# Dense products of a two-layer hybrid trunk: 520 tokens in parts of 240 and 280 instead of 260 and 260, five matmuls instead of six for each 128 by 128 weight block

## The chip, the cores and the metric

The kernel runs on one core of a Trainium2 chip. The metric is the device time of one execution in microseconds (us). The engines are named as in the profile: PE (TensorE; PEld is its loading of weights), DVE (VectorE), ACT (ScalarE), POOL (GpSimd), SP (SyncE). SBUF is the on-chip memory with 128 partitions, PSUM the memory that PE writes, here 8 banks of 512 float32 in each partition.

## The reference

Two decoder layers over 512 prompt tokens and 8 sample tokens, together 520 columns, all in float32. Cut to the dense products, which are what the change touches:

```python
def decoder_layer(x, ple, w, ...):
    h = rmsnorm(x, w['norm_ffn1'])
    x = x + 0.5 * swiglu(h, w['ffn1_w1'], w['ffn1_w3'], w['ffn1_w2'])   # 1024 -> 2816 (twice) -> 1024
    h = rmsnorm(x, w['norm_mix'])
    u = h @ w['w_in']                                                   # 1024 -> 5640
    dn_qkv, dn_z, dn_b, dn_a, da_q, da_k, da_v, gate_a, gate_b = split_in(u)
    ya = gated_delta_branch(...)                                        # convolution, L2 norms, scan
    yb = differential_attention(...)
    m = sigmoid(gate_a) * (ya @ w['w_a']) + sigmoid(gate_b) * (yb @ w['w_b'])
    x = x + m @ w['w_o']
    h = rmsnorm(x, w['norm_ffn2'])
    x = x + 0.5 * swiglu(h, w['ffn2_w1'], w['ffn2_w3'], w['ffn2_w2'])
    gate = sigmoid(rmsnorm(x, w['norm_ple']) @ w['w_ple_gate'])
    return x + gate * (ple @ w['w_ple'])
```

## The kernel before, in words

Activations stand transposed in SBUF, features on the partitions and the 520 tokens along the row: `X` is [128, 8, 520]. Every dense product is made of three products in the format fp32r: a float32 number is split into a high part (the same number written as fp32r) and a low part (what is left), for the activations (`Hh`, `Hl`; `Gh`, `Gl` of the FFN's hidden values; `Yh`, `Yl`; `Mh`, `Ml`; `PTh`, `PTl`) and for the weights (`whi`, `wlo`). The result is high weight by high activation, plus high weight by low activation, plus low weight by high activation, summed in PSUM. The 520 tokens do not fit one bank, so they are cut into two halves of `HT = 260`, each in a bank of its own. One weight block of 128 by 128 thus takes a set of six matmuls of 260 columns (`product`, L603 to L618; `block_low`, L643 to L667). `pair(b)` is the view of the two halves in banks b and b + 1, and `halves` cuts an SBUF row in the same way.

A weight block of the program is 128 x 2048 (8 chunks k by 256 columns): 16 sets, 96 matmuls, four banks. Two such blocks alternate between banks 0 to 3 and banks 4 to 7 (`block8`). In `block_low`, where other work needs banks 4 to 7, the two halves of a block use banks 0, 1 and banks 2, 3 and are released one by one (`half_done`, `half_evac`). The FFN's down products have 11 chunks by 128 columns, two of them to an output.

The order on each engine is written out by hand and every dependency is a semaphore. For each weight block SP loads `raw`, ACT writes `whi` (`hi`), DVE or POOL writes `wlo` (`lo`, L1665 on DVE) and PE waits for `split_done` (`split_ready`). PE also waits for `evac` (`banks_ready`) before it reuses banks. DVE empties the banks, in nearly all places by one instruction per output chunk: PSUM times `R`, the reciprocal root of the norm, into SBUF. Layer by layer the stages are: FFN 1 up (22 blocks, `ffn`), FFN 1 down (16 blocks of 66 matmuls), the convolution's six blocks of w_in (`to_u`, then nine DVE instructions per block, L1750 on), eight blocks by `block_low` with the L2 norms between them (`low_u`, L1780; `l2_norms`, L1795), the scan and the attention, eight gate blocks by `block_low` (`gate_half`, `head_norm`), w_a and w_b (`AB`, eight products of 48 matmuls), w_o (4 blocks), FFN 2, and the per-layer embedding (four products of 24 matmuls with `PTh`, then four blocks with the gate). DVE's `acc` holds the running sum of squares for the norms; `norm_rec` clears it after each use. The last chunk of layer 1 has its own loop (L1180 to L1187), by halves of 260.

Of the kernel before, what the change touches and what calls it, by code (L numbers as in the profile page):

```python
# [2353 lines left out]
```

## Time and profile before

| | |
|---|---|
| median of 3 runs | 2753.1 us (2751.6 to 2753.88) |
| the profiled execution (its span, first to last instruction) | 2749.5 us |
| PE matmuls | 2704.5 us busy, 98%, 23840 instructions |
| PE weight loads | 2566.3 us busy, 93%, 23840 |
| DVE | 1349.4 us, 49%, 1662 |
| ACT | 1021.9 us, 37%, 1168 |
| POOL | 241.2 us, 9%, 150 |
| DMA | 33.2% of 16 engines' span, 303.81 MB |

A matmul's time in the profile is its way from issue to the last result and overlaps the next ones: 282 ns each, although they start some 119 ns apart. So the mean duration is no cost; the distance from start to start is, and that is read from how many matmuls fill a stretch in which PE never idles. The 3.6 us between the profiled span and the median of the runs lie outside the instructions or between executions.

### The profile page before, as it was taken

How to read it: one execution, taken by the hardware profiler on the slowest of the kernel's cores; microseconds unless marked ns; L12 is line 12 of the kernel's file. 1: busy time of each engine (PE TensorE's matmuls, PEld its weight loads, DVE VectorE, ACT ScalarE, POOL GpSimd, SP SyncE). 2: the span in 40 equal slices, each digit the busy share in tenths (PEclk: the TensorE clock that was granted, in tenths of full speed). 3: DMA queues.
4: the chain of work that ended last, by engine and by line, in shares of the span. 5: the costliest groups of instructions: out<-in, count | busy, mean ns of one | idle time of the engine just before them, and what ended most of it. 6: DMA issues, size and time to landing. Idle time of an engine off the chain costs nothing.

```text
span 2749.5 us, 56360 instructions
## 1 busy us (share of the span) xinstructions
PE 2704.5 (98%) x23840; PEld 2566.3 (93%) x23840; DVE 1349.4 (49%) x1662; ACT 1021.9 (37%) x1168; POOL 241.2 (9%) x150
## 2 busy tenths in 40 slices
PE   8999999999999999999999999999999999999997
PEld 8999999976699999999999999999657999999997
DVE  5333347644676533333653333567356665333336
ACT  5333223412563333332343332333135534333223
POOL 0111000421000011100001100013210000111000
PEclk9999999999999999999999999999999999999998
DMA  4222232277422222222322222323873222222221
GB/s 159 93 92 73 94 119 95 94 228 249 151 81 89 93 92 92 87 85 89 108 92 92 92 79 93 124 91 100 269 240 104 93 93 81 93 92 85 87 95 66
DMA packets 119534, 303.81 MB, mean 110 GB/s; under 512 B 14946, under 2 KB 25186, under 8 KB 118882
## 3 DMA queue, kind: packets, MB, share of 16 engines
q1 hardware_dynamic: 119394, 301.79, 33.2%
q8 instruction: 106, 1.74, 0.3%
q14 instruction: 34, 0.28, 0.0%
HBM read 290.30 MB, written 11.44 MB: 110 GB/s over the span
## 4 chain that ended last, share of the span: by engine, by line
PE 93%; DVE 3%; ACT 2%; DVEq 2%; issue 1%; DMA 0%; SPq 0%; POOLq 0%; ACTq 0%
PE ps L614 69%; PE ps L662 13%; PE ps L829 2%; PE ps L916 1%; PE ps L982 1%; ACT sc L1230 1%; PE ps L897 1%; PE ps L883 1%; PE ps L715 1%; PE ps L1128 1%; DVEq L1799 0%; PE ps L964 0%; PE ps L710 0%; PE ps L935 0%; DVEq L1991 0%
## 5 line engine op out<-in xcount | busy, mean ns | idle before, releaser
L614 PE MATMUL ps<-Hh,whi 128*128 128x260 f32 x3440 | 691.9, 283 | 11.7 <-DVE Hl L1725 10.1
L614 PE MATMUL ps<-Hl,whi 128*128 128x260 f32 x3440 | 690.0, 282 | 0.0
L614 PE MATMUL ps<-Hh,wlo 128*128 128x260 f32 x3440 | 689.0, 282 | 0.0
L1230 ACT ACTIVATE whi<-raw 128x2048 fp32r<-128x2048 f32 (+2 forms) x225 | 396.0, 1760 | 780.2 <-PE ps L614 670.6
L1659 DVE TENSOR_TENSOR wlo<-raw,whi 128x2048 fp32r<-128x2048 f32 (+2 forms) x213 | 444.2, 2085 | 292.3 <-ACT whi L1230 292.2
L614 PEld LDWEIGHTS ps<-Hh,whi 128*128 128x128 f32 x3440 | 527.9, 188 | 12.8 <-issue 10.1
L614 PEld LDWEIGHTS ps<-Hl,whi 128*128 128x128 f32 x3440 | 530.2, 189 | 0.0
L614 PEld LDWEIGHTS ps<-Hh,wlo 128*128 128x128 f32 x3440 | 529.2, 188 | 0.0
L1230 ACT ACT_TABLE_LOAD x163 | 209.1, 1283 | 304.0 <-PE ps L614 233.4
L1659 DVE TENSOR_TENSOR ta<-ps,R 128x520 f32<-128x520 f32 x88 | 61.6, 700 | 475.8 <-PE ps L614 474.7
L614 PE MATMUL ps<-Gh,whi 128*128 128x260 f32 x1408 | 283.7, 283 | 0.0
L614 PE MATMUL ps<-Gh,wlo 128*128 128x260 f32 x1408 | 283.4, 282 | 0.0
L614 PE MATMUL ps<-Gl,whi 128*128 128x260 f32 x1408 | 282.7, 282 | 0.0
L1600 POOL TENSOR_TENSOR Gl<-tb,Gh 128x520 f32 x88 | 115.3, 1310 | 1594.1 <-ACT Gh L1230 1594.1
L614 PEld LDWEIGHTS ps<-Gl,whi 128*128 128x128 f32 x1408 | 217.2, 188 | 0.0
L614 PEld LDWEIGHTS ps<-Gh,whi 128*128 128x128 f32 x1408 | 216.8, 188 | 0.0
L614 PEld LDWEIGHTS ps<-Gh,wlo 128*128 128x128 f32 x1408 | 216.7, 188 | 0.0
L662 PE MATMUL ps<-Hh,whi 128*128 128x260 f32 x1024 | 212.8, 289 | 0.3 <-DVE U L1659 0.3
L662 PE MATMUL ps<-Hh,wlo 128*128 128x260 f32 x1024 | 206.1, 283 | 0.0
L662 PE MATMUL ps<-Hl,whi 128*128 128x260 f32 x1024 | 205.8, 283 | 0.0
L662 PEld LDWEIGHTS ps<-Hh,whi 128*128 128x128 f32 x1024 | 159.6, 189 | 4.5 <-issue 2.9
L662 PEld LDWEIGHTS ps<-Hh,wlo 128*128 128x128 f32 x1024 | 157.7, 188 | 0.0
(275 smaller groups left out, 2933.9 us busy)
## 6 DMA issues: line engine op xcount, KB each, us to landing
raw<-in_ffn_up SPq DMA_DIRECT2D x176, 512.0 KB, 4.2
raw<-in_ffn_down SPq DMA_DIRECT2D x128, 352.0 KB, 3.3
kb<-in_cache_k SPq DMA_DIRECT2D x128, 256.0 KB, 3.7
kb<-in_cache_v SPq DMA_DIRECT2D x128, 256.0 KB, 3.8
raw<-in_w_in SPq DMA_DIRECT2D x56, 512.0 KB, 4.4
raw<-in_w_gate SPq DMA_DIRECT2D x32, 512.0 KB, 4.8
raw<-in_w_ab SPq DMA_DIRECT2D x16, 512.0 KB, 4.4
raw<-in_w_o SPq DMA_DIRECT2D x16, 512.0 KB, 4.4
```

Source lines behind the costliest of these rows:

```text
L614: last = nc.tensor.matmul(ps[:, bank + 2 * m + c, 0:HT], w, x[:, k0 + k, c * HT:(c + 1) * HT], start=starts and k == 0 and n == 0, stop=st ...
L662: last = nc.tensor.matmul(ps[:, 2 * m + c, 0:HT], w, x[:, k, c * HT:(c + 1) * HT], start=k == 0 and t == 0, stop=k == KD - 1 and t == 2)
L715: return nc.tensor.matmul(out, in_, CC[0:rows, C_ID:C_ID + rows], start=True, stop=True)
L829: last = nc.tensor.matmul(ps[part(h % 2), bank, cell(x, h)], lhs[part(h % 2), cell(x, h)], rhs(part(h % 2), cell(x, h)), start=x == 0 and ...
L883: last = nc.tensor.matmul(ps[:, 3, o:o + 2], st[b][:, s, h * P:(h + 1) * P], dq[:, 4 * b + s, h, :], start=True, stop=True)
L897: nc.tensor.matmul(ps[:, 3, :], bkm[:, s, :], Uz[:, :, :].rearrange("p h c -> p (h c)"), start=True, stop=True).then_inc(s_pe.on(f"o{b}{s} ...
L916: last = nc.tensor.matmul(ps[32 * h:32 * h + 32, 6, :].rearrange("p (g k) -> p g k", g=4), qz[:, s * P + 32 * h:s * P + 32 * h + 32], kb[t ...
L982: last = nc.tensor.matmul(ps[:, 7, t * P:SEQ], vtok[:, h % 2, t * P:(t + 1) * P], aT[:, t, t * P:SEQ], start=t == 0, stop=t == 3)
L1128: last = nc.tensor.matmul(ps[:, 4 + 2 * (k % 2) + c, 0:HT], ones, tb[:, k % 2, c * HT:(c + 1) * HT], start=True, stop=True)
L1230: return nc.scalar.activation(out, in_, func, **kw)
L1600: nc.gpsimd.tensor_tensor(col(Gl, 2 * i + p), tb[:, p, :], col(Gh, 2 * i + p).bitcast(F32), ALU.subtract).then_inc(gl_done, 1)
L1659: return V.tensor_tensor(out, a_, b_, op)
```

## The change

Tokens are cut into the first `N0 = 240` and the other 280. The high and the low activations of a product now stand in one tensor (`Hs`, `Gs`, `YMs`, `PTs`, at the addresses that they had), so one matmul of 480 columns takes the first 240 tokens of both: the high weight by high and by low activation, to two neighbouring stretches of one bank. Only one of the two stretches is the place where the sum is built; the other is added to it later, by DVE. The set of one 128 by 128 weight block is five matmuls with 480 + 280 + 280 + 240 + 280 = 1560 columns, where it was 6 x 260 = 1560. The 480-column matmul is the first of a set that opens an accumulation and the last of all others. `fold` is the new DVE work: it copies the stretch of 240 columns (for one or two output chunks) from PSUM to SBUF and adds it to the sum in PSUM, with a drain after each. Where the result goes to `X` (down products, w_o) there is no `fold` but one more addition of 240 columns per chunk. `acc` serves as `fold`'s buffer between norms, so its clearing moves from `norm_rec` to the places before the next sum. The main row of 520 tokens is now contiguous over two banks (columns 272 to 511 and 0 to 279). Nothing is changed on SP, POOL or in the number of ACT instructions. The last chunk's own loop (L1180) is left as it was.

```diff
+N0 = 240
+BANK = 512
+AT = BANK - N0
...
         def pair(b):
-            return ps[:, b:b + 2, 0:HT]
...
+            return ps[:, b:b + 2, :].rearrange("p a c -> p (a c)")[:, AT:AT + T]
...
+            def five(h, l, x, bank, start, stop):
+
+                xs, hk, lk = x
+                low, n1 = abs(lk - hk), T - N0
+                first, top_ = min(hk, lk), AT - N0 if hk < lk else AT
+
+                def both():
+                    return nc.tensor.matmul(ps[:, bank, AT - N0:BANK].rearrange("p (a c) -> p a c", a=2), h,
+                                            xs[:, first:first + low + 1:low, 0:N0], start=start, stop=stop)
+
+                if start:
+                    last = both()
+                nc.tensor.matmul(ps[:, bank + 1, 0:n1], h, xs[:, hk, N0:T], start=start, stop=False)
+                nc.tensor.matmul(ps[:, bank + 1, 0:n1], h, xs[:, lk, N0:T], start=False, stop=False)
+                nc.tensor.matmul(ps[:, bank, top_:top_ + N0], l, xs[:, hk, 0:N0], start=False, stop=False)
+                last = nc.tensor.matmul(ps[:, bank + 1, 0:n1], l, xs[:, hk, N0:T], start=False, stop=stop)
+                if not start:
+                    last = both()
+                return last
...
-                        for n, (w, x) in enumerate(((h, rh), (h, rl), (l, rh))):
-                            for c in range(2):
-                                last = nc.tensor.matmul(ps[:, bank + 2 * m + c, 0:HT], w,
-                                                        x[:, k0 + k, c * HT:(c + 1) * HT],
-                                                        start=starts and k == 0 and n == 0,
-                                                        stop=stops and k == ks - 1 and n == 2)
+                        last = five(whi[:, slot, o:o + P], wlo[:, slot, o:o + P], rx(k0 + k), bank + 2 * m,
+                                    starts and k == 0, stops and k == ks - 1)
...
+            low_parts = acc[:, 0:2 * N0].rearrange("p (a c) -> p a c", a=2)
+
+            def fold(b, n=1, by=low_parts):
+
+                x = ps[:, b:b + 2 * n:2, AT:BANK]
+                V.tensor_copy(by[:, 0:n, :], ps[:, b:b + 2 * n:2, AT - N0:AT])
+                dve.drain()
+                TT(x, x, by[:, 0:n, :], ALU.add)
+                dve.drain()
...
                         done(L, nb + m)
 
+                        fold(4 * p, 2)
                         dve.wait_ge(gl_done, L * 2 * KF + m + (hid * KF + 1))
-                        TT(halves(ta[:, p, :]), pair(4 * p), halves(R[:, :]), ALU.mult).then_inc(ta_ready, 1)
-                        TT(halves(tb[:, p, :]), pair(4 * p + 2), halves(R[:, :]), ALU.mult).then_inc(evac, 1)
+                        TT(ta[:, p, :], pair(4 * p), R[:, :], ALU.mult).then_inc(ta_ready, 1)
+                        TT(tb[:, p, :], pair(4 * p + 2), R[:, :], ALU.mult).then_inc(evac, 1)
...
-                        V.scalar_tensor_tensor(out=halves(Xc(m)), in0=pair(4 * p), scalar=0.5, in1=halves(Xc(m)),
+                        x0 = X[:, bass.ds(m, 1), 0:N0].rearrange("p o t -> p (o t)")
+                        V.scalar_tensor_tensor(out=x0, in0=ps[:, 4 * p, AT - N0:AT], scalar=0.5, in1=x0, op0=ALU.mult, op1=ALU.add)
+                        dve.drain()
+                        V.scalar_tensor_tensor(out=Xc(m), in0=pair(4 * p), scalar=0.5, in1=Xc(m),
                                                op0=ALU.mult, op1=ALU.add).then_inc(evac, 1)
...
-                        TT(halves(U[:, u + m, :]), pair(2 * m), halves(R[:, :]), ALU.mult).then_inc(evac if m else half_evac, 1)
+                        fold(2 * m)
+                        TT(U[:, u + m, :], pair(2 * m), R[:, :], ALU.mult).then_inc(evac if m else half_evac, 1)
```

`fold(4 * p, 2)` or `fold(2 * m)` is added in the same way in `to_u`, `gate_half`, the w_a and w_b loop, the embedding's products and its gate.

PE, the first weight block of the program, around the sum of squares (`acc` by the ones in `CC`): before,

```order
L614 MATMUL ps<-Hl,whi 128x260 x2
L614 MATMUL ps<-Hh,wlo 128x260 x2
L674 MATMUL ps<-acc,CC 128x260 x2
L614 MATMUL ps<-Hh,whi 128x260 x2
L614 MATMUL ps<-Hl,whi 128x260 x2
```

and of the change:

```order
L616 MATMUL ps<-Hs,whi 128x480
L708 MATMUL ps<-acc,CC 128x240
L708 MATMUL ps<-acc,CC 128x280
L621 MATMUL ps<-Hs,whi 128x280
L622 MATMUL ps<-Hs,whi 128x280
L623 MATMUL ps<-Hs,wlo 128x240
L624 MATMUL ps<-Hs,wlo 128x280
```

Three pairs of 260 columns became one matmul of 480, three of 280 and one of 240.

DVE, in the stretch of the L2 norms (`ta` holds a root, `U` the projections): before,

```order
L1828 TENSOR_SCALAR gg<-ax 128x20
L1798 RECIPROCAL ta<-ta 128x520
L1800 SCALAR_TENSOR_TENSOR U<-U,ta 128x520
L1798 RECIPROCAL ta<-ta 128x520
L1800 SCALAR_TENSOR_TENSOR U<-U,ta 128x520
L1659 TENSOR_TENSOR U<-ps,R 128x520 x2
L1659 TENSOR_TENSOR gg<-gg,sp 128x20
```

and of the change:

```order
L1850 SCALAR_TENSOR_TENSOR U<-U,ta 128x520
L1706 COPY acc<-ps 128x240
L1691 TENSOR_TENSOR ps<-ps,acc 128x240
L1691 TENSOR_TENSOR U<-ps,R 128x520
L1706 COPY acc<-ps 128x240
L1691 TENSOR_TENSOR ps<-ps,acc 128x240
L1691 TENSOR_TENSOR U<-ps,R 128x520
L1691 TENSOR_TENSOR gg<-gg,sp 128x20
```

Each emptying of a half block is now three instructions, and they still stand behind the same two reciprocals.

## Rows read from the trace of the kernel before

**Rows 1.** The page: busy time of each engine; the chain, by engine

```profile
PE 2704.5 (98%) x23840; PEld 2566.3 (93%) x23840; DVE 1349.4 (49%) x1662; ACT 1021.9 (37%) x1168; POOL 241.2 (9%) x150
PE 93%; DVE 3%; ACT 2%; DVEq 2%; issue 1%; DMA 0%; SPq 0%; POOLq 0%; ACTq 0%
```

**Rows 2.** The page's groups of matmuls (count; busy us, mean ns; idle before)

```profile
L614 PE MATMUL ps<-Hh,wlo 128*128 128x260 f32 x3440 | 689.0, 282 | 0.0
...
L614 PE MATMUL ps<-Gh,wlo 128*128 128x260 f32 x1408 | 283.4, 282 | 0.0
...
L662 PE MATMUL ps<-Hh,wlo 128*128 128x260 f32 x1024 | 206.1, 283 | 0.0
```

**Rows 3.** The chain in order of time: start us, us, what

```profile
1383.40 378.30 PE ps L614 x3168
...
2304.62 387.07 PE ps L614 x3240
```

**Rows 4.** Timeline of PE and PEld, short streams and plain float32: start, length

```profile
588.85 0.97 PEld L883 LDWEIGHTS ps<-dq,st 128*128 128x128 f32 x8 [0.84 <-issue]
...
507.61 1.04 PE L733 MATMUL ps<-tb,CC 128*128 128x260 f32 x4
```

**Rows 5.** Groups of those: duration min/median/max of loads and matmuls

```profile
L883 PEld LDWEIGHTS ps<-dq,st x128: 186/192/192, 584.8 to 1988.9; 128*128 128x128 f32 x128
...
L733 PE MATMUL ps<-tb,CC x64: 381/382/487, 493.0 to 1901.5; 128*128 128x260 f32 x64
```

**Rows 6.** Groups of DVE by form, for the price of `fold`

```profile
L1892 DVE COPY Tm<-ps 128x512 f32<-128x512 f32 x20 | 13.8, 692 | 43.0 <-PE ps L829 42.9
...
L1659 DVE TENSOR_TENSOR st<-st,ps 128x512 f32<-128x512 f32 x16 | 11.0, 687 | 16.4 <-PE ps L897 16.4
...
L1975 DVE COPY Pz<-ps 128x256 f32<-128x256 f32 x2 | 0.8, 424 | 4.6 <-PE ps L926 4.6
```

**Rows 7.** Timeline of DVE, FFN up and its end (start, length, idle before)

```profile
266.07 0.70 DVE L1659 TENSOR_TENSOR ta<-ps,R 128x520 f32<-128x520 f32 x1 [5.11 <-PE ps L614]
...
267.93 2.29 DVE L1659 TENSOR_TENSOR wlo<-raw,whi 128x2048 fp32r<-128x2048 f32 x1 [0.56 <-ACT whi L1230]
```

**Rows 8.** Timeline of POOL, the last low part of the hidden values

```profile
271.96 1.32 POOL L1600 TENSOR_TENSOR Gl<-tb,Gh 128x520 f32 x1 [8.67 <-ACT Gh L1230]
```

**Rows 9.** Timeline of DVE, the convolution's blocks

```profile
428.18 1.31 DVE L1659 TENSOR_TENSOR U<-ps,R 128x520 f32 x2 [0.28 <-PE ps L614]
...
439.58 1.30 DVE L1659 TENSOR_TENSOR U<-ps,R 128x520 f32 x2 [1.79 <-PE ps L614]
```

**Rows 10.** Timeline of DVE and then PE, the L2 norms

```profile
502.33 4.13 DVE L1828 TENSOR_SCALAR gg<-ax 128x20 f32<-128x20 f32 x1 [0.50 <-issue]
...
514.57 1.30 DVE L1659 TENSOR_TENSOR U<-ps,R 128x520 f32<-128x520 f32 x2
...
515.41 0.48 PE L662 MATMUL ps<-Hh,whi 128*128 128x260 f32 x2 [0.16 <-DVE U L1659]
```

**Rows 11.** Busy us by stretch: PE, PEld, DVE, ACT, POOL; clock; DMA

```profile
500.00:556.00 56.00, 55.84 (x456) 53.54 (x452) 48.96 (x50) 25.41 (x32) 18.42 (x4) 1.00 0.21 77
```

**Rows 12.** Timeline of DVE and PE from the last gate to w_a and w_b

```profile
845.56 2.29 DVE L1659 TENSOR_TENSOR wlo<-raw,whi 128x2048 fp32r<-128x2048 f32 x1
...
847.90 0.50 PE L614 MATMUL ps<-Yh,whi 128*128 128x260 f32 x2 [0.33 <-DVE wlo L1659]
```

**Rows 13.** Timeline of DVE, two products of w_b in a row

```profile
859.71 1.31 DVE L1659 TENSOR_TENSOR sg<-ps,sg 128x520 f32<-128x520 f32 x2 [4.46 <-PE ps L614]
...
868.17 2.28 DVE L1659 TENSOR_TENSOR wlo<-raw,whi 128x2048 fp32r<-128x2048 f32 x1
```

**Rows 14.** Timeline of DVE, the embedding's products

```profile
1321.35 2.29 DVE L1659 TENSOR_TENSOR wlo<-raw,whi 128x2048 fp32r<-128x2048 f32 x1 [0.64 <-ACT whi L1230]
```

**Rows 15.** Timeline of PE and DVE, layer 0 to 1, then the end

```profile
1377.95 0.51 PE L614 MATMUL ps<-Hh,whi 128*128 128x260 f32 x2 [0.21 <-DVE Hl L2196]
...
2719.80 1.31 DVE L1659 TENSOR_TENSOR pg<-ps,R 128x520 f32<-128x520 f32 x2 [2.52 <-PE ps L614]
```

More of the change, by code:

```diff
@@ L659, in block_low @@
                             pe.wait_ge(hl_done, L * KD + k + 1)
-                        for t, (w, x) in enumerate(((h, Hh), (h, Hl), (l, Hh))):
-                            for c in range(2):
-                                last = nc.tensor.matmul(ps[:, 2 * m + c, 0:HT], w, x[:, k, c * HT:(c + 1) * HT],
-                                                        start=k == 0 and t == 0, stop=k == KD - 1 and t == 2)
+                        last = five(h, l, Hx(k), 2 * m, k == 0, k == KD - 1)
                     last.then_inc(block_done if m else half_done, 1)
@@ L673, in norm_sum @@
                 for c in range(2):
-                    last = nc.tensor.matmul(ps[:, 6 + c, 0:HT], ones, acc[:, c * HT:(c + 1) * HT], start=True, stop=True)
+                    last = nc.tensor.matmul(cut(6, c), ones, acc[:, tok(c)], start=True, stop=True)
                 last.then_inc(sum_ready, 1)
@@ L1239, in norm_root @@
                 act.wait_ge(sum_ready, L * NORMS + (nj + 1))
-                A_(halves(R[:, :]), pair(6), ACT.Sqrt, scale=1.0 / D, bias=eps).then_inc(rt_ready, 1)
+                A_(R[:, :], pair(6), ACT.Sqrt, scale=1.0 / D, bias=eps).then_inc(rt_ready, 1)
             def x_ready(L, u):
@@ L1323, in l2_root @@
                         act.wait_ge(l_dve.sem, l_dve.at(f"n{p}", L, i - 1))
-                    A_(halves(ta[:, p, :]), pair(4), ACT.Sqrt, bias=eps).then_inc(l_act.sem, 1)
+                    A_(ta[:, p, :], pair(4), ACT.Sqrt, bias=eps).then_inc(l_act.sem, 1)
                 act.drain()
@@ L1714, in to_u @@
                 done(L, n)
+                fold(4 * p, 2)
                 for q in range(2):
-                    last = TT(halves(col(U, c + q)), pair(4 * p + 2 * q), halves(R[:, :]), ALU.mult)
+                    last = TT(col(U, c + q), pair(4 * p + 2 * q), R[:, :], ALU.mult)
                 last.then_inc(evac, 1)
@@ L2158, in _ @@
                         x = sg[:, j, 2 * i + q, :]
-                        last = TT(halves(x), pair(4 * (t % 2) + 2 * q), halves(x), ALU.mult)
+                        last = TT(x, pair(4 * (t % 2) + 2 * q), x, ALU.mult)
                     last.then_inc(evac, 1)
@@ L2172, in _ @@
                     for q in range(2):
+                        x0 = X[:, 2 * i + q, 0:N0]
+                        TT(x0, ps[:, 4 * (i % 2) + 2 * q, AT - N0:AT], x0, ALU.add)
+                    dve.drain()
+                    for q in range(2):
                         m = 2 * i + q
-                        last = TT(halves(Xc(m)), pair(4 * (i % 2) + 2 * q), halves(Xc(m)), ALU.add)
+                        last = TT(Xc(m), pair(4 * (i % 2) + 2 * q), Xc(m), ALU.add)
                     last.then_inc(evac, 1)
@@ L2186, in _ @@
                         dve.wait_ge(a_done, L * 6 + 5 + i // 2)
+                    fold(4 * (i % 2), 2, pf)
                     for q in range(2):
-                        last = V.tensor_copy(halves(pu[:, 2 * i + q, :]), pair(4 * (i % 2) + 2 * q))
+                        last = V.tensor_copy(pu[:, 2 * i + q, :], pair(4 * (i % 2) + 2 * q))
                     last.then_inc(evac, 1)
@@ L2205, in _ @@
                     done(L, B_PLE + 2 + i)
+                    fold(4 * (i % 2), 2, pf)
                     for q in range(2):
-                        last = TT(halves(pg[:, i % 2, q, :]), pair(4 * (i % 2) + 2 * q), halves(R[:, :]), ALU.mult)
+                        last = TT(pg[:, i % 2, q, :], pair(4 * (i % 2) + 2 * q), R[:, :], ALU.mult)
                     last.then_inc(evac, 1)
@@ L2218, in _ @@
                 dve.wait_ge(ple_half, L + 1)
-                TT(halves(pg[:, 1, 0, :]), pair(4), halves(R[:, :]), ALU.mult).then_inc(pg_ready, 1)
+                fold(4, by=pf)
+                TT(pg[:, 1, 0, :], pair(4), R[:, :], ALU.mult).then_inc(pg_ready, 1)
                 if L + 1 < DEPTH:
@@ L2230, in _ @@
                     done(L, B_PLE + 5)
-                    TT(halves(pg[:, 1, 1, :]), pair(6), halves(R[:, :]), ALU.mult).then_inc(evac, 1)
+                    fold(6, by=pf)
+                    TT(pg[:, 1, 1, :], pair(6), R[:, :], ALU.mult).then_inc(evac, 1)
                     low(2)
```

83 lines of the change are left out of this document (49 added, 34 removed).

## The prediction

> **What bounds the kernel now.** I read the page's totals first: PE is busy for 98% of the span, and the chain that ended last is PE for 93% of it [rows 1]. DVE has 49% and is never the bound over the whole. Then the page's groups of matmuls: nearly all of PE's instructions are the sets of six that the change rewrites. By the low weights, two of which belong to each set, there are (3440 + 1408 + 1024) / 2 = 2936 sets [rows 2], and by the code 128 for w_a and w_b, 128 for w_o and 32 for the embedding: 3224 sets. The last chunk's loop keeps its form. Next the chain in order of time, because a mean duration of 282 ns says nothing of the pace: 3240 matmuls stand in 387.07 us and 3168 in 378.30 us, 119.5 and 119.4 ns each, without a hole [rows 3]. A set takes 6 x 119.5 = 717 ns, all sets 2312 us of 2749.5. So the question is what these 119.5 ns are made of.
>
> Streaming 260 columns at 2.4 GHz takes 108.3 ns. 11.2 ns are something else. Two stretches tell what it may be. Eight weight loads before matmuls of only 2 columns fill 0.97 us, and one load lasts 192 ns [rows 4, 5]: (970 - 192) / 7 = 111 ns from load to load, with next to nothing to stream. That is a floor of about 111 ns per matmul set by the weight load alone, and 108.3 ns of stream lie just under it. Four plain float32 matmuls of 260 columns fill 1.04 us at 382 ns each [rows 4, 5]: (1040 - 382) / 3 = 219 ns, which is two passes of 108.3 ns and 3 ns more. Where the stream is long, the load is hidden and only 3 ns are lost. I read the 119.5 ns as a load of 111 ns that can't quite hide behind 108 ns of stream, plus some 8 ns of handing over between the two.
>
> **The change part by part.** *Products.* Columns stay at 1560 per set; loads go from six to five, and one matmul becomes long. 480 columns: 200.0 + 3 = 203 ns, as in the long streams. 280 columns: 116.7 + 3 = 119.7 ns if the load is now hidden, up to 119.7 + 8 = 127.7 if the handing over stays; I take 122, nearer to the first, since the stream is now longer than the load. 240 columns: the load binds, 111 to 119.5 ns; I take 119.5, what is seen at 260. Sum 203 + 3 x 122 + 119.5 = 688.5 ns, 28.5 less than 717. Bounds: 203 + 359 + 111 = 673 (44 less) and 203 + 383 + 119.5 = 705.5 (11.5 less). That is with the load as the cause; the other causes are rivals below.
>
> *DVE.* A `fold` is a copy from PSUM and an addition in PSUM. Copies of 512 and 256 columns took 692 and 424 ns, an addition with PSUM of 512 took 687 [rows 6]; so 480 columns cost about 655 and 240 about 405 ns each. With a drain (about 0.08 us) after each, a `fold` of two chunks is 1.5 us and of one chunk 1.0 us. By the code there are 130 of the first kind, 67 of the second and 48 single additions of 240 columns: some 195 + 67 + 23 = 285 us of DVE, which lie beside PE and cost nothing where DVE has room. In FFN up it has: a block is 11.0 us of PE, DVE works 4.4 us in it and then 5.9. Nothing there waits. I went through the places where it has none, per layer:
>
> - Last FFN up block, both FFNs: `Gl` ends at 273.28, 7.2 us after the block's end at 266.07 [rows 7, 8], and PE needs it after 11 sets, 7.9 us before and 7.6 now. `fold` takes 1.5 us, of which 0.56 was idle time before `wlo` [rows 7]. It comes at 8.1: a wait of 0.5 us, 1 us a layer.
> - Convolution: DVE starts two blocks 11.40 us apart with 1.79 idle [rows 9]: 9.6 us of work, and with `fold` 11.1. PE needs 16 x 0.688 = 11.0. They run level, and the lag from the reciprocal at the start is no longer caught up: 1.5 us.
> - L2 norms: the narrowest place. In 56 us DVE is busy for 49 [rows 11]. From 502.33 to 514.57 it works through `gg` and two reciprocals, then empties both halves of a block, and PE waits 0.16 us for the first of them already, until 515.41 [rows 10]. With a `fold` ahead of it that release is 1.0 us later while PE arrives 0.5 earlier. Each of the four blocks there has at least 8.2 us of norms (514.57 less 506.4), 1.4 of emptying, 2.0 of `fold`, 0.5 small: 12 us and more against 11.0. DVE decides the pace. Working it through block by block, the stage ends some 3.5 us later than before, and its 64 sets save nothing.
> - Last gate to w_a: DVE's gate evacuation and `wlo`, which PE waits 0.33 us for at 847.90 [rows 12], come 1.0 later: 1.7 us with the bank's release.
> - w_a and w_b: in a pair of products DVE goes from 859.71 over an addition, `wlo`, `Ml` and the next emptying to the next `wlo`, which ends at 870.45 [rows 13]; two `fold`s put 3.0 us into it, where PE has a margin of about 0.8. Waits of 0.8, 2.1, 0.9 and 0.5: 4.3 us.
> - Embedding: products of 24 matmuls, 2.75 us on PE, with 2.8 us of emptying each and 2.29 of `wlo` [rows 14] for every second: 3.5 us.
> - Layer end: PE waits 0.21 us for the last `Hl` at 1377.95 [rows 15] and it comes 3.4 later: 3 us. At the program's end the way from 2719.80 [rows 15] to the end is DVE and ACT: one `fold` of each kind, 2.4 us, and 8 sets save nothing.
>
> Sum 2 x (1 + 1.5 + 3.5 + 1.7 + 4.3 + 3.5) + 3 + 2.4 = 36 us. I don't see any of these waits in the trace yet, so bounds: 15 (idle pieces absorb more than I think, and other engines hold) to 60 (drains dearer, lags carried on). The clearing of `acc`, 0.5 us of DVE moved, is nothing beside that. Loads of weights move with `split_done`; DMA is at a third and no wait names it.
>
> **Sum.** Sets that save: 3224 - 2 x 64 - 16 = 3080. 3080 x 28.5 ns = 88 us, bounds 35 and 136. Less 36: a gain of 52. Profiled span 2749.5 - 52 = 2698; the median of the runs is 3.6 above the span, so 2753.1 - 52 = 2701 us.
>
> **Rivals.** *Pace per column, slower.* The extra time may belong to the columns: 119.5 - 3 = 116.5 ns for 260, 0.448 ns a column, if the one-pass format can't be read faster. For it: every one-pass product here has 260 columns, so the trace can't exclude it. Against it: the load floor of 111 ns, which would lie so near by chance. Then a set saves one fixed cost of 3 ns, 3080 x 3 = 9 us, the waits on DVE cost about 32, and the kernel takes 2753 + 23 = 2776 us. This decides from 36 / 3080 = 12 ns of saving per set downwards.
> The Trainium skill, "TensorE: Matmul & The Clock Gate", section "Back-to-back issue gap", speaks for a small saving too: a matmul is N / 2.4 + 2.5 ns. By that rule 260 columns take 110.8 ns where this trace has 119.5, and a set would save 2.5 ns, a kernel of about 2777 us. Since the rule misses the pace of these very matmuls by 9 ns, I give it no more than the rival's chance. The page's section "LDWEIGHTS (loading the stationary operand)" has 128 / 1.2 = 107 ns for a load; the rows say 111.
>
> *A fixed cost per matmul.* 11.2 ns go with each of the six. A set saves 11.2 ns, 34 us in all, and DVE takes as much: 2755 us. Against it: only 3 ns in the long streams of rows 4.
>
> *Short or long one-pass streams fall to two passes.* Plain float32 shows 219 ns for 260 columns [rows 4], so two paces exist; if 240 columns got the slower one, they would take 203 instead of 119.5: 3080 x 83.5 = 257 us, 2701 + 257 = 2958 us. Nothing in the trace ties the pace to the width.
>
> *Fuller gain.* The load is hidden behind 280 columns and the waits are half of mine: 2753 - 136 + 20 = 2637, with middle values 2655 us.
>
> *DVE costs double.* Products as forecast, waits 72: 2737 us.
>
> **How the numbers follow.** Forecast 0.58, fuller gain 0.13, DVE costs double 0.05, fixed cost 0.05, per column 0.15, two passes 0.04. Likeliest 2701 us. The bounds of its own terms give 2660 to 2745. The range of 8 in 10 goes from 2650 into the fixed-cost rival at 2755; the per-column and two-pass cases are left out, and the far end of the fuller gain. A measurement of this kernel tells a difference of 0.2%, 5.5 us. Faster: forecast, fuller gain and double costs, 0.76. Same: the fixed cost and edges, 0.07. Slower: 0.17.
>
> **What would show it.** Right: in an FFN stage the chain holds 80 matmuls per block at about 11.0 us, the load groups five to a set; the 480-column matmul starts 203 ns before its follower, the others 119 to 122 ns. FFN blocks shorter by 0.45 us, the L2 stage longer by about 3.5 us, w_a and w_b with waits of PE for `wlo`, DVE at some 1620 us busy. Wrong: a set of 714 ns (per column) or 706 ns (fixed) in FFN up, where DVE is far from binding; or a 240-column matmul with 200 ns to the next. If sets are at 688 and the total is still above 2720, it is DVE's stages that I priced too low.

## The result, and the profile after

The changed kernel takes 2793.3 us (median of 4 runs, 2790.8 to 2795.6), the kernel before beside it on the same chip 2753.5 us. The ratio is 1.0144, with a 95% interval of 1.013 to 1.0159: 1.4% slower. The forecast was 2701 us with a range up to 2755. The profiled execution took 2793.8 us, its span is 2792.0 us.

The page of the changed kernel, first the busy times and the chain (they answer to [rows 1]), then groups of matmuls (count; busy us, mean ns; idle before):

```profile
PE 2718.5 (97%) x20616; PEld 2477.4 (89%) x20616; DVE 1587.7 (57%) x2104; ACT 1031.3 (37%) x1168; POOL 241.0 (9%) x150
...
PE 83%; DVE 8%; DVEq 5%; ACT 2%; issue 2%; DMA 0%; POOL 0%; SPq 0%; POOLq 0%; ACTq 0%
...
L616 PE MATMUL ps<-Hs,whi 128*128 128x480 f32 x2232 | 836.2, 384 | 22.4 <-DVE Hs L1774 10.5
...
L623 PE MATMUL ps<-Hs,wlo 128*128 128x240 f32 x2232 | 609.7, 273 | 0.0
```

3224 matmuls are gone, yet PE is busy for 14 us more, and PE's share of the chain fell from 93% to 83%: what it lost, DVE and its queue gained. So two things are to be found: why fewer matmuls save nothing, and what DVE costs.

First the pace where nothing waits. The same stage, FFN 2 up of layer 0, as a stretch of 200 us, of the kernel before and then of the changed one (us; then PE, PEld, DVE, ACT, POOL with counts; clock; DMA):

```profile
960.00:1160.00 200.00, 200.00 (x1682) 200.00 (x1682) 76.05 (x70) 77.87 (x72) 22.39 (x18) 1.00 0.27 90
```

```profile
970.00:1170.00 200.00, 200.00 (x1398) 191.98 (x1397) 96.86 (x106) 77.07 (x70) 23.55 (x18) 1.00 0.28 95
```

Two matmuls of such a count are those under way when the stretch begins. Before, 1680 matmuls are 280.0 sets of six: 714.3 ns a set. After, 1396 are 279.2 sets of five: 716.3 ns. The set did not get 28.5 ns shorter; it got 2 ns longer. PEld is busy for only 192 of 200 us now, and that spare time is worth nothing.

In FFN down the balance is slightly better. 100 us of FFN 1 down of layer 0, before and then changed:

```profile
280.00:380.00 100.00, 100.00 (x835) 100.00 (x834) 34.26 (x32) 26.10 (x27) 0.00 (x0) 1.00 0.28 92
```

```profile
280.00:380.00 100.00, 100.00 (x700) 95.76 (x699) 35.71 (x39) 25.79 (x26) 0.00 (x0) 1.00 0.29 96
```

Before, 833 matmuls are 720.3 ns a set; after, 698 are 716.3 ns. So a set of six at 260 columns is some 6 ns dearer here than in FFN up (120.0 and 119.0 ns a matmul; why is open), and the change saves 4 ns where in FFN up it loses 2.

Then the places where PE waits. The first blocks by halves, after the convolution's blocks, in the timeline of PE (start, length, idle before and who ended it), then the same place as stretches:

```profile
474.89 0.39 PE L616 MATMUL ps<-Hs,whi 128*128 128x480 f32 x1
478.21 0.74 PE L616 MATMUL ps<-Hs,whi 128*128 128x480 f32 x1 [2.94 <-DVE U L1691]
478.75 0.43 PE L621 MATMUL ps<-Hs,whi 128*128 128x280 f32 x1
478.98 0.43 PE L622 MATMUL ps<-Hs,whi 128*128 128x280 f32 x1
479.21 0.40 PE L623 MATMUL ps<-Hs,wlo 128*128 128x240 f32 x1
```

```profile
474.00:478.00 4.00, 1.27 (x9) 0.91 (x7) 3.28 (x7) 1.26 (x2) 0.07 (x1) 1.00 0.66 251
478.00:481.00 3.00, 2.79 (x11) 2.68 (x12) 2.53 (x8) 0.00 (x0) 0.00 (x0) 0.51 0.03 8
482.00:486.00 4.00, 4.00 (x30) 3.80 (x29) 0.33 (x2) 3.89 (x12) 0.00 (x0) 1.00 0.28 42
```

PE idles for 2.94 us, and then the granted clock is 0.51 for the next 3 us, that is 1.2 GHz: 11 matmuls stand in 3 us where 21 would at full clock. The wait costs its own length and then about half of the 3.4 us that follow. At w_a and in the embedding waits of 1.81 us are also followed by half clock, about 1 us after their end:

```profile
852.42 0.46 PE L616 MATMUL ps<-YMs,whi 128*128 128x480 f32 x1 [1.81 <-issue]
...
1337.26 0.46 PE L616 MATMUL ps<-PTs,whi 128*128 128x480 f32 x1 [1.81 <-DVE pu L2246]
```

```profile
853.00:857.00 4.00, 4.00 (x20) 3.83 (x19) 3.93 (x3) 2.43 (x3) 0.00 (x0) 0.57 0.02 4
1338.00:1342.00 4.00, 4.00 (x19) 3.78 (x19) 3.93 (x5) 0.00 (x0) 0.00 (x0) 0.57 0.08 33
```

DVE in the convolution's blocks (start, length):

```profile
415.18 2.28 DVE L1691 TENSOR_TENSOR wlo<-raw,whi 128x2048 fp32r<-128x2048 f32 x1
...
420.55 0.65 DVE L1706 COPY acc<-ps 128x480 f32<-128x480 f32 x1
421.28 0.67 DVE L1691 TENSOR_TENSOR ps<-ps,acc 128x480 f32<-128x480 f32 x1
422.11 1.31 DVE L1691 TENSOR_TENSOR U<-ps,R 128x520 f32 x2 [0.17 <-issue]
...
426.25 2.29 DVE L1691 TENSOR_TENSOR wlo<-raw,whi 128x2048 fp32r<-128x2048 f32 x1
...
475.99 0.40 DVE L1706 COPY acc<-ps 128x240 f32<-128x240 f32 x1
476.47 0.42 DVE L1691 TENSOR_TENSOR ps<-ps,acc 128x240 f32<-128x240 f32 x1
477.36 0.70 DVE L1691 TENSOR_TENSOR U<-ps,R 128x520 f32<-128x520 f32 x1 [0.48 <-issue]
```

A block takes DVE 11.07 us, with gaps of 0.2 us only, where [rows 9] had 1.79 us idle. The price of a `fold` was forecast well: 0.65 + 0.67 us and two drains, 1.5 us from its start to the next instruction. The last three lines are the `fold` and the emptying of the first half block, for which PE waits until 478.21; without DVE's added work the emptying begins at 474.35 us.

### The profile page after: what moved, and what is told of

It reads as the page before. It is cut to its first block, busy times and chain, and to the rows that moved or that the text cites. A ratio compares the mean times of both kernels' runs of the same rounds, so it can differ in the third digit from the quotient of the medians.

```text
span 2792.0 us, 50817 instructions
## 1 busy us (share of the span) xinstructions
PE 2718.5 (97%) x20616; PEld 2477.4 (89%) x20616; DVE 1587.7 (57%) x2104; ACT 1031.3 (37%) x1168; POOL 241.0 (9%) x150
## 4 chain that ended last, share of the span: by engine, by line
PE 83%; DVE 8%; DVEq 5%; ACT 2%; issue 2%; DMA 0%; POOL 0%; SPq 0%; POOLq 0%; ACTq 0%
PE ps L616 22%; PE ps L624 13%; PE ps L621 13%; PE ps L622 13%; PE ps L623 11%; PE ps L862 2%; DVE wlo L1691 2%; DVEq L1825 1%; PE ps L949 1%; DVE ps L1691 1%; DVEq L1849 1%; DVEq L1707 1%; PE ps L1015 1%; ACT sc L1262 1%; PE ps L930 1%
## 5 line engine op out<-in xcount | busy, mean ns | idle before, releaser
L616 PE MATMUL ps<-Hs,whi 128*128 128x480 f32 x2232 | 836.2, 384 | 22.4 <-DVE Hs L1774 10.5
L624 PE MATMUL ps<-Hs,wlo 128*128 128x280 f32 x2232 | 657.1, 294 | 0.0
L621 PE MATMUL ps<-Hs,whi 128*128 128x280 f32 x2232 | 653.9, 293 | 1.9 <-DVE Hs L2254 1.3
L622 PE MATMUL ps<-Hs,whi 128*128 128x280 f32 x2232 | 651.2, 292 | 0.0
L623 PE MATMUL ps<-Hs,wlo 128*128 128x240 f32 x2232 | 609.7, 273 | 0.0
L622 PEld LDWEIGHTS ps<-Hs,whi 128*128 128x128 f32 x2232 | 420.4, 188 | 61.1
L616 PEld LDWEIGHTS ps<-Hs,whi 128*128 128x128 f32 x2232 | 417.6, 190 | 27.8 <-issue 25.3
L621 PEld LDWEIGHTS ps<-Hs,whi 128*128 128x128 f32 x2232 | 421.2, 189 | 9.0 <-DVE Hs L2254 2.2
L624 PEld LDWEIGHTS ps<-Hs,wlo 128*128 128x128 f32 x2232 | 421.4, 189 | 0.0
L623 PEld LDWEIGHTS ps<-Hs,wlo 128*128 128x128 f32 x2232 | 421.2, 189 | 0.0
L616 PE MATMUL ps<-Gs,whi 128*128 128x480 f32 x704 | 263.3, 380 | 0.0
L621 PE MATMUL ps<-Gs,whi 128*128 128x280 f32 x704 | 205.3, 292 | 1.8 <-POOL Gs L1632 1.8
L624 PE MATMUL ps<-Gs,wlo 128*128 128x280 f32 x704 | 205.5, 292 | 0.0
L622 PE MATMUL ps<-Gs,whi 128*128 128x280 f32 x704 | 205.1, 291 | 0.0
L622 PEld LDWEIGHTS ps<-Gs,whi 128*128 128x128 f32 x704 | 132.5, 188 | 20.4
L621 PEld LDWEIGHTS ps<-Gs,whi 128*128 128x128 f32 x704 | 132.6, 188 | 3.8 <-issue 3.0
```

The costliest lines, as they stand in the source:

```text
L616: return nc.tensor.matmul(ps[:, bank, AT - N0:BANK].rearrange("p (a c) -> p a c", a=2), h, xs[:, first:first + low + 1:low, 0:N0], start=s ...
L621: nc.tensor.matmul(ps[:, bank + 1, 0:n1], h, xs[:, hk, N0:T], start=start, stop=False)
L622: nc.tensor.matmul(ps[:, bank + 1, 0:n1], h, xs[:, lk, N0:T], start=False, stop=False)
L623: nc.tensor.matmul(ps[:, bank, top_:top_ + N0], l, xs[:, hk, 0:N0], start=False, stop=False)
L624: last = nc.tensor.matmul(ps[:, bank + 1, 0:n1], l, xs[:, hk, N0:T], start=False, stop=stop)
```

## The experiments

Ten kernels. The first three take the change apart, the next three measure the matmul by itself, two try another cut of the tokens, and two put DVE's cost in its place. In the texts written ahead of the runs theory A is a pace per column, B the forecast's load and handing over, C a fixed cost on each matmul.

**Parts alone: six matmuls, no work for DVE.** The high and the low activation go to the same place.

```diff
 def both():
-    return nc.tensor.matmul(<480 columns to two stretches>)
+    nc.tensor.matmul(ps[:, bank, AT:BANK], h, xs[:, hk, 0:N0], start=start, stop=False)
+    return nc.tensor.matmul(ps[:, bank, AT:BANK], h, xs[:, lk, 0:N0], start=False, stop=stop)
 # and no fold, no second addition to X
```

> Parts of 240 and 280 tokens, but six matmuls a set: the high and the low activation of the first 240 tokens in two matmuls to the same place, so DVE has nothing to add up (no fold, no second addition to X); the whole computation is done. Theory A (0.448 ns a column and 3 ns): 3 x 110.5 + 3 x 128.4 = 716.7 ns a set against 717 before: the time of before, 2753 within 3 us. Theory B (load floor and handing over): 3 x 119.5 + 3 x 122 = 724.5 ns, some 24 us longer, 2777 us. Theory C: 717, no change.

Measured 2770.7 us against 2752.6, ratio 1.0069 (1.0055 to 1.0083). All three theories missed; parts of 240 and 280 cost 18 us by themselves. The stretch of FFN 2 up:

```profile
960.00:1160.00 200.00, 200.00 (x1662) 200.00 (x1661) 73.80 (x70) 74.50 (x68) 23.61 (x18) 1.00 0.28 95
```

1660 matmuls are 276.7 sets, 722.9 ns each. Theory B's 724.5 is near it, but with the wrong parts, as the widths show below. Over all stages it is 18.1 us / 3224 = 5.6 ns a set, so elsewhere less than the 8.6 ns of FFN up.

**Five matmuls, no work for DVE.**

```diff
 def fold(b, n=1, by=low_parts):
+    return
 # and no second addition to X
```

> The changed kernel without the vector engine's added work: no fold and no second addition to X, so the low activation's share of the first 240 tokens is left out of the outputs (in some products the high one's). Theory A (the set of five saves 3 ns at most, the loss is in waits on DVE): all of the waits go, 2793 less 39 = 2754 us, or 2744 if the 3 ns are saved. Theory B (a set of 688.5 ns): 2753 - 88 = 2665 us. If it stayed near 2793, the matmuls themselves and not DVE would have cost the time.

Measured 2752.2 us against 2752.6, ratio 0.9999 (0.999 to 1.0008). With DVE's added work taken away, nothing is left of the loss and nothing has been won: theory A without its 3 ns, and not B's 2665. PE in the same stretch has the count of the changed kernel:

```profile
960.00:1160.00 200.00, 200.00 (x1398) 191.98 (x1397) 76.07 (x70) 77.45 (x72) 22.28 (x17) 1.00 0.26 89
```

**Six matmuls, all of DVE's work.**

```diff
 def both():
+    nc.tensor.matmul(ps[:, bank, AT - N0:AT], h, xs[:, first, 0:N0], start=start, stop=False)
+    return nc.tensor.matmul(ps[:, bank, AT:BANK], h, xs[:, first + low, 0:N0], start=False, stop=stop)
```

> The changed kernel with its 480-column matmul cut into two of 240 columns, to the same two stretches of the bank; DVE's work is as in the changed kernel and the computation is whole. Theory A: one fixed cost of 3 ns more per set, 2793 + 10 at the most, less where DVE's waits hide it: 2793 to 2803 us. Theory C (11.2 ns a matmul): 2793 + 3224 x 11.2 ns = 2829 us at most, some 2815 with the waits absorbing a part. Theory B: 2 x 119.5 instead of 203, 36 ns a set: 2890 us at most.

Measured 2810.7 us, ratio 1.021 (1.0196 to 1.0224): above theory A's 2803 at most, below C's 2815 and far below B's 2890. Together the four make a square, in us against 2752.6 or, for the change itself, 2753.5:

| | without DVE's work | with it | DVE's work |
|---|---|---|---|
| 240/280, six matmuls | 2770.7 | 2810.7 | 40.0 |
| 240/280, five matmuls | 2752.2 | 2793.3 | 41.1 |
| merging two matmuls | -18.5 | -17.4 | |

The effects add up: parts +18, merging -18, DVE's work +41. Merging saves 18.5 us / 3224 = 5.7 ns a set, more than theory A's 3 ns; the widths show why.

**Widths.** The six matmuls of a set in another width in each FFN stage: 240, 280, 480 and 480 as two rows in FFN up, the others in FFN down.

```diff
-last = nc.tensor.matmul(ps[:, bank + 2 * m + c, 0:HT], w, x[:, k0 + k, c * HT:(c + 1) * HT], ...)
+last = nc.tensor.matmul(ps[:, bank + 2 * m + c, 0:W], w, x[:, k0 + k, x0:x0 + W], ...)
```

> The kernel before, with the sets of six high-and-low matmuls of each FFN stage given another width (the numbers that come out are not the reference's there): FFN up 240, 280, 480, and 480 read as two rows of 240 (layer 0 first and second FFN, layer 1 first and second); FFN down 512, 320, 400, 360. The distance from matmul to matmul is read in each stage. Theory A, a pace per column of 0.448 ns and 3 ns: 110.5, 128.4, 218, 218; 232, 146, 182, 164 ns. Theory B, my forecast's (a weight load of 111 ns with 8 ns of handing over, otherwise 1/2.4 ns a column and 3 ns): 119.5, 122, 203, 203; 216, 136, 170, 153 ns. Theory C, a fixed 11.2 ns on each matmul beside 1/2.4 ns a column: 111.2 (or the load's floor), 127.9, 211.2, 211.2; 224.5, 144.5, 177.9, 161.2 ns.

Stretches inside the stages of 240, 512, 280, 320, 480, 400, 480 as two rows, and 360 columns:

```profile
50.00:250.00 200.00, 200.00 (x1782) 200.00 (x1780) 81.05 (x76) 84.50 (x76) 23.55 (x18) 1.00 0.27 91
265.00:490.00 225.00, 225.00 (x971) 182.04 (x971) 39.54 (x36) 29.41 (x29) 0.00 (x0) 1.00 0.15 48
1075.00:1300.00 225.00, 225.00 (x1760) 225.00 (x1759) 78.18 (x74) 80.43 (x73) 23.70 (x18) 1.00 0.24 81
1320.00:1460.00 140.00, 140.00 (x958) 140.00 (x957) 39.63 (x37) 29.41 (x30) 0.00 (x0) 1.00 0.22 70
1560.00:1960.00 400.00, 400.00 (x1842) 345.36 (x1841) 81.66 (x76) 85.32 (x77) 25.00 (x19) 1.00 0.14 47
1975.00:2150.00 175.00, 175.00 (x964) 174.98 (x963) 39.23 (x36) 29.30 (x29) 0.00 (x0) 1.00 0.19 62
2735.00:3135.00 400.00, 400.00 (x1831) 343.62 (x1831) 81.64 (x76) 85.35 (x77) 24.98 (x19) 1.00 0.14 47
3150.00:3310.00 160.00, 160.00 (x974) 160.00 (x973) 39.62 (x37) 29.39 (x30) 1.15 (x1) 1.00 0.20 65
```

Time by count, less the two under way: 112.4 ns for 240 columns, 128.0 for 280, 146.4 for 320, 164.6 for 360, 181.9 for 400, 217.4 and 218.7 for 480, 232.2 for 512. From 280 to 512 that is 104.2 ns for 232 columns, 0.449 ns a column, and 2.3 ns are left over: theory A. B's 203 for 480 and 216 for 512 are out by 14 to 16 ns, C's 211 and 224 by 6 to 8. The 512 columns ran in FFN down; within FFN up (280 and 480) the line is 0.447 ns a column and 2.8. At 240 either line gives 110.1 and 112.4 is seen. Three matmuls of 240 and three of 280 make 721.2 ns by these rows, 6.9 above the 714.3 of before: three times the 2.3 ns by which 240 columns lie above the line. That is most of what the parts alone cost in FFN up (8.6 ns a set; the other 1.7 stay open). Merging then takes two of these three matmuls away: 2 x 112.4 - 218.7 = 6.1 ns, near the 5.7 of the square. So the change saves one fixed cost of about 2.3 ns and pays it back with the one 240-column matmul that is left.

**Formats and short streams.** The moving operand in bf16, side by side or 4 bytes apart; 64 weight columns; short fp32r streams.

```diff
+out, wt, xx = ps[0:wc, b, 0:W], w[:, 0:wc], x[:, kk, x0:x0 + W]
+if kind == "bf16":
+    wt, xx = CC[:, 0:wc // 2].bitcast(B16), CC[:, 0:W // 2].bitcast(B16)
+if kind == "bf16 every second":
+    wt, xx = CC[:, 0:wc // 2].bitcast(B16), CC[:, 0:W].bitcast(B16)[:, 0:2 * W:2]
```

> The kernel before, with the six high-and-low matmuls of a set given another form in each FFN stage (their numbers are not the reference's). FFN up, layer 0 first and second FFN: 260 columns with 64 weight columns instead of 128; 260 columns of bf16 with bf16 weights. Layer 1: 480 columns of bf16; 260 columns of bf16 read 4 bytes apart. FFN down: 128, 64, 200, 160 columns of fp32r with 128 weight columns. Theory A (0.449 ns a column of fp32r and 2.6 ns, with a floor of 111 ns from the weight load): 64 weight columns change nothing, 119.5; the down stages show the floor, 111 to 112 for 64, 128, 160 and 200 columns. If the pace belongs to the format (4 bytes a column), bf16 shows 110 to 111 ns at 260 and 202 at 480 columns; if it belongs to the pitch of the reading, bf16 at 4 bytes apart shows 119.5 and bf16 side by side 111; if it belongs to PE's clock or to PSUM, all bf16 forms stay at 119 and 217. Theory B (load of 111 and handing over of 8 ns): with 64 weight columns the load is shorter and 260 columns fall to 111; 480 bf16 columns as fp32r ones, 217.

Stretches of 260 columns with 64 weight columns; 128 columns; 260 in bf16; 480 in bf16; 200 columns; 260 in bf16 at 4 bytes apart:

```profile
55.00:255.00 200.00, 200.00 (x1690) 200.00 (x1689) 75.56 (x70) 75.84 (x70) 23.62 (x18) 1.00 0.27 91
275.00:380.00 105.00, 105.00 (x942) 105.00 (x942) 37.26 (x35) 29.06 (x29) 0.00 (x0) 1.00 0.31 103
960.00:1160.00 200.00, 200.00 (x1807) 176.57 (x1805) 81.68 (x76) 84.86 (x77) 23.27 (x18) 1.00 0.27 91
...
1480.00:1840.00 360.00, 360.00 (x1779) 173.94 (x1778) 78.68 (x74) 81.55 (x74) 23.18 (x18) 1.00 0.15 51
1865.00:1970.00 105.00, 105.00 (x943) 105.00 (x942) 37.26 (x35) 28.94 (x29) 0.00 (x0) 1.00 0.32 103
2555.00:2755.00 200.00, 200.00 (x1738) 165.88 (x1736) 77.38 (x72) 80.30 (x73) 23.37 (x18) 1.00 0.27 91
```

118.5 ns with half of the weight columns: theory B expected 111 and falls. 128 and 200 columns take 111.7 and 111.6: there is a floor that does not depend on the columns, as the loads of [rows 4] had it, and it lies below the 260 columns' pace without making it. 260 bf16 columns take 110.8 ns and 480 take 202.6, that is 1/2.4 ns a column and 2.5. The same 260 at 4 bytes apart take 115.2, between what a pure matter of format (111) and a pure matter of pitch (119.5) would give. So the slow pace belongs neither to PE's clock nor to PSUM, which are the same for bf16, but to the moving operand. (The Trainium skill, "TensorE: Matmul & The Clock Gate", section "Back-to-back issue gap", gives N / 2.4 + 2.5 ns for an isolated matmul: the bf16 rows agree to 0.1 ns, although they stand in an unbroken stream, for which the section has about 131 ns at 512 columns; the fp32r rows agree with neither.)

**Reading.** Other addresses and pitches for the same six matmuls.

```diff
+if kind in ("same row", "same block and row"): xx = x[:, 0, x0:x0 + W]
+if kind in ("same block", "same block and row"): wt = (wlo if n == 2 else whi)[:, slot, at:at + P]
+if kind == "8 bytes apart": xx = x[:, kk, 0:2 * W:2]
+if kind == "first tokens": xx = x[:, kk, 0:W]
```

> The kernel before, with the six matmuls of a set reading from elsewhere in each FFN stage (their numbers are not the reference's). FFN up: the same weight block and the same chunk of tokens for all 8 chunks; the same weight block only; the same chunk only; 260 tokens read 8 bytes apart. FFN down: both halves read the first 256, 264 or 260 tokens (no offset), and in layer 1's second FFN 260 tokens 8 bytes apart. In the run before, 260 bf16 columns took 110.8 ns side by side and 115.2 ns at 4 bytes apart, and fp32r ones 119.5. If the pace is one of reading bytes or pitch, the rows 8 bytes apart take clearly more than 119.5 (124 or up to twice as much), and the fixed rows nothing less. If it is the address in SBUF (offsets, or changing rows), the fixed ones and those without an offset fall towards 111 ns. If it belongs to the fp32r format whatever is read, all stages of 260 show 119 to 120, 8 bytes apart too, and 256 and 264 show 117.6 and 121.2.

Same block and row; 256 columns; same block; 264 columns; same row; 260 columns in FFN down; 8 bytes apart:

```profile
50.00:250.00 200.00, 200.00 (x1716) 200.00 (x1716) 77.36 (x72) 79.52 (x72) 23.59 (x18) 1.00 0.27 91
275.00:375.00 100.00, 100.00 (x849) 100.00 (x848) 33.88 (x32) 26.11 (x27) 0.00 (x0) 1.00 0.30 97
960.00:1160.00 200.00, 200.00 (x1683) 200.00 (x1682) 76.36 (x71) 78.96 (x71) 22.30 (x17) 1.00 0.26 88
1190.00:1300.00 110.00, 110.00 (x906) 110.00 (x905) 36.86 (x36) 27.49 (x29) 0.00 (x0) 1.00 0.27 88
1400.00:1600.00 200.00, 200.00 (x1717) 200.00 (x1716) 77.35 (x72) 79.52 (x72) 23.64 (x18) 1.00 0.27 91
1625.00:1735.00 110.00, 110.00 (x919) 110.00 (x918) 35.89 (x36) 27.93 (x28) 0.00 (x0) 1.00 0.30 98
2310.00:2740.00 430.00, 430.00 (x1855) 384.34 (x1854) 82.94 (x78) 85.84 (x78) 26.37 (x20) 1.00 0.14 47
```

8 bytes apart, 260 columns take 232.1 ns: 0.884 ns a column where side by side it is 0.449, nearly the same time per byte passed over, 0.110 and 0.112 ns. That speaks for a rate of reading. A chunk read again and again takes 116.7 instead of 119.0 ns; what those 2.3 ns are stays open. The bf16 forms all read one fixed stretch of `CC`, so they had this advantage too. If the parts add up, the 8.2 ns between bf16 side by side (110.8) and fp32r (119.0) are 4.4 of pitch, 2.3 of changing chunks and 1.5 that no run explains. The timeline shown above adds a witness: at the granted clock of one half, 280 columns go from 478.98 to 479.21, 0.23 us, which is one column per cycle of 1.2 GHz. Where PE itself is slow enough, reading seems to keep up.

**Parts of 256 and 264**, merged to 512 columns; all else as changed.

```diff
-N0 = 240
+N0 = 256
```

> The changed kernel with parts of 256 and 264 tokens in place of 240 and 280: the merged matmul has 512 columns, a whole bank, and nothing else changes but the widths of DVE's folds. By the widths run (0.449 ns a column and 2.6 ns, the 240-column ones held at 112.4 by the weight load): 232.1 + 3 x 121.1 + 117.5 = 713 ns a set where the changed kernel has 717.8 in FFN up and down, 3224 x 4.8 = 15 us less, and 16 more columns in each fold cost DVE 0.02 us each, most of it hidden: 2779 us, between 2775 and 2785. If the pace of the 240-column matmul is not held by the load, no change: 2793.

Measured 2795.2 us (2790.3 to 2797.9), ratio 1.0151 (1.0136 to 1.0167): no gain over the change's 1.0144, where 2779 was expected. The stretch has 1397 matmuls, 715.8 ns a set, not 713: as the changed kernel with its 716.3. The rows of 256, 264 and 512 columns make 232.2 + 3 x 121.7 + 118.1 = 715.4, but they stand in FFN down, where 260 columns take 120.0 ns, and this stretch in FFN up, where they take 119.0; so that agreement is partly luck. Sets of mixed widths come out 1 to 3 ns above the sum of their widths (716.3 against 218.7 + 3 x 128.0 + 112.4 = 715.1 in the changed kernel, 722.9 against 721.2 in the parts alone), and no run says why.

```profile
970.00:1170.00 200.00, 200.00 (x1399) 187.62 (x1397) 98.53 (x105) 75.56 (x69) 23.59 (x18) 1.00 0.27 95
```

**The merged matmul in the FFN stages only**, with 256 and 264, where DVE has room; elsewhere as in the parts alone.

```diff
 def both():
+    if not merged[0]:
+        nc.tensor.matmul(ps[:, bank, AT:BANK], h, xs[:, hk, 0:N0], start=start, stop=False)
+        return nc.tensor.matmul(ps[:, bank, AT:BANK], h, xs[:, lk, 0:N0], start=False, stop=stop)
     return nc.tensor.matmul(<512 columns>)
 # merged[0] is set in ffn; folds outside it are gone
```

> Parts of 256 and 264, the 512-column matmul and DVE's added work in the FFN stages only; in all other stages six matmuls, high and low activation of the first 256 tokens to the same place, no fold and no second addition. The whole computation is done. By the widths run a merged set is 713 ns and an unmerged one 3 x 117.5 + 3 x 121.1 = 716 ns, where the kernel before has 717.6: 2112 FFN sets x 4.6 = 10 us and 1112 x 1.6 = 2 us saved, and DVE gives back 2 us at the last FFN up blocks: 2753 - 10 = 2743 us, between 2740 and 2750. If the saving of a merged set were nothing beside the waits, 2755.

Measured 2756.0 us against 2752.1, ratio 1.0014 (1.0005 to 1.0023): a little slower, where 2743 was expected. The forecast took the 713 ns for a merged set, and no set ran at that. It was the one version the runs pointed to; the kernel before remains the best.

**DVE's work taken out of the convolution's blocks alone.**

```diff
 def to_u(L, n, c, p):
     done(L, n)
-    fold(4 * p, 2)
```

> The changed kernel without the fold in the convolution's blocks of w_in alone (to_u, 6 blocks a layer): those outputs lack one activation part for the first 240 tokens. The prediction put 1.5 us a layer on this place: 2793 - 3 = 2790 us. Read from the traces, the stretch from the conv blocks to the end of the first blocks by halves is 4.7 us a layer longer than without any fold, with one wait of PE of 2.9 us at its end; if that wait is the lag that the convolution's folds pile up, it goes: 2793 - 9 = 2784 us, and the wait of 2.9 us is gone from the trace. If it is the fold of the first half block itself, 1.0 us, it shrinks by a third only.

Measured 2784.1 us, ratio 1.0117 (1.01 to 1.0134), 9.2 less than the change and as the lag's 2784 has it. The same place has no wait and no half clock now:

```profile
469.00:473.00 4.00, 4.00 (x30) 3.81 (x29) 3.81 (x4) 0.00 (x0) 1.11 (x2) 1.00 0.09 15
473.00:477.00 4.00, 4.00 (x27) 3.54 (x26) 3.50 (x7) 1.26 (x2) 0.00 (x0) 1.00 0.63 247
477.00:481.00 4.00, 4.00 (x31) 3.85 (x30) 3.00 (x11) 0.04 (x1) 0.00 (x0) 1.00 0.02 6
```

So six folds of 1.5 us a layer, none of which PE waits for in its own block, pile up a lag that is paid behind them, with the clock on top. The two layers' stages there are 8.9 us shorter in this trace than in the changed kernel's.

**DVE's work taken out of w_a, w_b and the embedding's products.**

```diff
-                    fold(4 * (t % 2), 2)
...
-                    fold(4 * (i % 2), 2, pf)
```

> The changed kernel without the folds of w_a and w_b (8 a layer) and of the embedding's four products (4 a layer), whose outputs lack one activation part for the first 240 tokens. The prediction put 4.3 and 3.5 us a layer on these: 2793 - 15.6 = 2778 us. The traces show 4.4 and 3.8 us a layer against the kernel without any fold, 2793 - 16.4 = 2777 us, if nothing is carried on. If the waits only move on (w_o and the FFN after it are still there to take a lag), 2785 or more.

Measured 2782.2 us (2777.0 to 2783.0), ratio 1.0109 (1.0092 to 1.0126). The profiled run took 2777.0, as expected, but three of four runs took 2782 to 2783, so the gain is 11 us by the median, between the expected 16 and the 8 or less of waits that move on. The traces tell the two apart: the stages from w_a to w_o and the embedding's products are 12.5 us shorter than in the changed kernel, and 4.6 us of the profiled run's gain lie in the scan and the attention, whose instructions are the same in both kernels.

## Why the prediction was wrong, point by point

- **The failed step is the cause of the 119.5 ns.** I read it as "a load of 111 ns that can't quite hide behind 108 ns of stream, plus some 8 ns of handing over". It is a pace per column: 0.449 ns of fp32r, with 2.3 ns for the matmul. The floor exists (111.6) but by an estimate from these rows it only binds below about (111.6 - 2.3) / 0.449 = 243 columns, so it speaks against a 240-column part, where I had it speak for the 280-column one. The 3 ns per matmul were nearly right. By term of the sum: 480 columns 203 forecast, 218 measured; 280 columns 122, 128.0; 240 columns 119.5, 112.4. The set came to 716 instead of 688.5 ns, and 88 us of saving became 0.4: that is, 2752.2 against 2752.6 us. The prediction's own sign for a pace per column was a set of 714 ns in FFN up; 716 came.
- **Why I believed it.** Every fp32r product before had 260 columns, so the trace fitted both theories with two numbers. I drew the 3 ns and the pace of 1/2.4 ns from plain float32, 219 ns for two passes [rows 4, 5]. Its passes run at 108 ns each, fp32r's at 119: the operand format that was measured was not the one in question. The per-column rival was written down with its price, 2776 us, and given 0.15. It had the mechanism of the pace, and yet the kernel took 17 us more: the 9 us that it still let the sets save did not come, because 240 columns lie above the line, and DVE cost 41 us instead of its 32.
- **DVE's waits in sum were nearly right**: 36 forecast, 41.1 measured (40.0 in the other pair). By place, both layers together, as the length of the stages in the changed kernel's trace less that in the trace of five matmuls without DVE's work (spans 2792.0 and 2750.7 us, so 41.3 in all):

| place | forecast us | measured us |
|---|---|---|
| last FFN up block (`Gl`) | 2 | 2.8 |
| convolution, first half blocks | 3 | 9.5 |
| L2 norms, up to the scan | 7 | 6.0 |
| last gate, w_a and w_b, w_o | 12 | 9.9 |
| embedding's products | 7 | 7.5 |
| layer end; program end | 3; 2.4 | 2.7; 2.4 |
| scan and attention; program start | none | 1.9; -1.6 |

The last row is no work of DVE's: scan and attention are 3.0 us longer in layer 0 and 1.0 shorter in layer 1, where the stretches at half clock fall differently in the two traces.

- **The mechanism that I left out is the clock behind a wait.** Beside the 2.94 us of idle time the convolution's place holds 3.4 us at half clock, 1.7 us lost; 2.94 + 1.7 = 4.6 of its 4.7 us a layer. There are five such stretches in the dense products of the changed kernel that the one without DVE's work lacks (at 478, 853, 1338, 1860 and 2717 us), 8.5 us in all. They follow five of the six waits of 1.81 to 3.02 us in the dense products; the sixth, 1.81 us at 2232.77, and four of 1.36 to 1.40 us kept the full clock. Nor is a place bound to it: in the run without the convolution's folds the same wait of 1.81 us at w_a was followed by a granted clock of 1.00. In the other direction I had PE arrive 0.5 us earlier per block; it did not, so some of the waits became smaller than in my sum, and the clock filled the gap. That the totals meet, 36 and 41, is therefore luck in part.
- **The convolution.** "They run level" was nearly right for the pace (11.07 us of DVE against 11.46 of PE), but the lag from the reciprocal could shrink by only 0.4 us a block and came due in the first half block, where I had priced only 1.5 us. The run without folds there gave back 9.2 us.
- **Hidden work** was right where DVE is idle: FFN 2 up of layer 0 takes 253.15 us with the folds and 253.15 without. So DVE's additional reading and writing of PSUM does not slow the matmuls either. DVE is busy for 1587.7 us, not for some 1620: the drains were priced, and they do not count as busy.

## What to carry to other kernels

Before a time per instruction is split into causes, look whether the trace holds the same instruction in a second size; if it doesn't, the split is a guess, and one run with several widths settles it. When all operations of a kind have one size, fewer and larger ones bring only the fixed part: here 2.3 ns of 119, and even that is lost if one of the new sizes falls under a floor. Price a new wait of PE with what may follow it: here the granted clock was halved for 3.4 us, 1.7 us lost, after five of the six longest waits before the end of the program. And where an engine works without idle time through several blocks, look for the place at which its lag is collected.
